# Blocked products over twelve chunks instead of eight, in a streaming attention step on one Trainium2 core

## What is computed

```python
z = einsum('bld,dc->blc', h, w_in)             # fq fk fv fg ff sq sk sv sg
fo = forgetting_attention(fq, fk, fv, lf) * silu(fg)       # 16 heads of 64
so = sliding_window_attention(sq, sk, sv, sinks, rel_bias) * silu(sg)   # 16 heads, 4 key/value heads
out = einsum('blc,cd->bld', concat([fo, so]), w_out)
y = layer_norm(ALPHA * h + out)
```

## Time and profile before

| | |
|---|---|
| median of 3 runs | 1018.74 us (1018.06 to 1019.41) |
| the profiled execution, its own time | 1019.1 us |
| its span in the trace | 1017.6 us, 1.5 us less than its time |
| TensorE busy | 998.6 us, 98% |
| VectorE busy | 715.2 us, 70% |
| ScalarE busy | 531.7 us, 52% |
| granted TensorE clock, mean | 0.996 of full speed |

### The profile page before, as it was taken

One profiled execution on the slowest core, in us unless ns is written; L12 is line 12 of the kernel. 1 busy time (PEld: TensorE's weight loads), 2 busy tenths in 40 slices (PEclk: granted clock), 3 DMA queues, 4 the chain that ended last, 5 costly groups with the idle time before them and its releaser, 6 DMA issues.

```text
span 1017.6 us, 20277 instructions
## 1 busy us (share of the span) xinstructions
PE 998.6 (98%) x7283; PEld 937.3 (92%) x7283; DVE 715.2 (70%) x1423; ACT 531.7 (52%) x1217; POOL 81.5 (8%) x156
## 2 busy tenths in 40 slices
PE   9999999999999999999999999999999999999995
PEld 6899999999999999999999999999999888888884
DVE  6988686776868677686767787668787655141685
ACT  5556465565645556464655676556677562111400
POOL 1620101001010100001010000000000000000000
PEclk9999999999999999999999999999999999999998
DMA  9142333223233323234321222231226443222423
GB/s 347 57 134 100 117 112 130 90 96 108 94 125 110 126 67 103 98 106 140 111 95 60 91 81 98 98 105 56 85 82 249 173 175 104 83 82 82 166 68 118
DMA packets 36258, 115.06 MB, mean 113 GB/s; under 512 B 9312, under 2 KB 9728, under 8 KB 33584
## 3 DMA queue, kind: packets, MB, share of 16 engines
q1 hardware_dynamic: 24208, 87.00, 24.8%
q0 software_dynamic: 11856, 27.14, 7.9%
q10 hardware_dynamic: 144, 0.26, 0.1%
HBM read 99.31 MB, written 18.29 MB: 116 GB/s over the span
## 4 chain that ended last, share of the span: by engine, by line
PE 86%; DVE 6%; DMA 4%; issue 2%; ACT 2%; SPq 1%; DVEq 0%; ACTq 0%
PE ps L1642 28%; PE ps L1652 25%; PE ps L1895 20%; PE ps L1860 5%; PE ps L1834 4%; DMA w_raw<-in_w_all 2%; PE ps L1818 2%; PE ps L1817 2%; DMA x_raw<-in_xT 2%; DVE wl L1118 1%; DVE tb L1295 1%; PE ps L1880 1%; SPq L582 0%; PE ps L1838 0%; ACT pt L961 0%
## 5 line engine op out<-in xcount | busy, mean ns | idle before, releaser
L1642 PE MATMUL ps<-xh,wh 128*128 128x296 f32 (+1 forms) x860 | 258.8, 301 | 0.2 <-DVE xl L1366 0.2
L1642 PE MATMUL ps<-xh,wl 128*128 128x296 f32 (+1 forms) x860 | 254.8, 296 | 0.0
L1642 PE MATMUL ps<-xl,wh 128*128 128x296 f32 (+1 forms) x860 | 254.6, 296 | 0.0
L1895 PE MATMUL ps<-wh,mix_parts 128*128 128x512 f32 x576 | 184.1, 390 | 0.0
L1642 PEld LDWEIGHTS ps<-xh,wh 128*128 128x128 f32 x860 | 161.8, 188 | 3.8 <-DVE xl L1366 1.8
L1642 PEld LDWEIGHTS ps<-xl,wh 128*128 128x128 f32 x860 | 161.9, 188 | 0.0
L1642 PEld LDWEIGHTS ps<-xh,wl 128*128 128x128 f32 x860 | 161.5, 188 | 0.0
L1118 DVE TENSOR_TENSOR wl<-w_raw,wh 128x1024 fp32r<-128x1024 f32 (+1 forms) x150 | 143.0, 953 | 19.8 <-ACT wh L853 8.5
L939 ACT ACTIVATE tb<-tb,small 128x256 f32<-128x256 f32 (+5 forms) x160 | 81.3, 508 | 92.2 <-DVE small L1314 64.2
L1895 PEld LDWEIGHTS ps<-wh,mix_parts 128*128 128x128 f32 x576 | 108.2, 188 | 22.3
L1895 PE MATMUL ps<-wl,mix_parts 128*128 128x512 f32 x320 | 124.5, 389 | 0.0
(11 more groups left out here) (198 smaller groups left out, 1737.3 us busy)
## 6 DMA issues: line engine op xcount, KB each, us to landing
w_raw<-in_w_all SPq DMA_DIRECT2D x106, 512.0 KB, 4.5
w_raw<-in_w_all SPq DMA_DIRECT2D x14, 1024.0 KB, 4.8
cbc<-c_rows POOLq DMA_DIRECT2D x16, 360.0 KB, 4.1
x_raw<-in_xT SPq DMA_DIRECT2D x7, 592.0 KB, 11.7
rows<-in_x_p POOLq DMA_DIRECT2D x4, 1024.0 KB, 5.2
out_y_p<-rows SPq DMA_DIRECT2D x16, 256.0 KB, 2.5
mix_rows<-mixT POOLq DMA_DIRECT2D x14, 288.0 KB, 2.4
rel_copies<-rel_rows POOLq DMA_DIRECT2D x8, 384.0 KB, 10.5
```

What stands on the lines that cost most here:

```text
L1642: ins = nc.tensor.matmul(ps[:, bank, result(tile, h)], a[f][:, w], b[:, ko, first:first + width], start=(ko == n_first and i == 0), stop=( ...
L1895: ins = nc.tensor.matmul(ps[:, bank, :], a, b[slot][:, w], start=(ko == 0 and i == 0), stop=(ko == KO - 1 and i == len(products) - 1))
```

## The change

The blocks now cover 12 chunks (CUT = 6) and 4 are plain. A block product has 18 matmuls and is issued as three pieces of 6; a plain unit has 6. A duo is still 15 units, in 29 pieces (UNIT_PIECES), and all steps are counted in pieces. The unit order after 7 changes: 8 is "four", 9 and 10 plain tile 0 late, 11 and 12 plain tile 1 early.

The x sums grow to 6 chunks each. Sum seven stays in SBUF; six and three share one buffer, `sum_both`: both are stored to DRAM in the opening and each is fetched again in every duo from 2 on, three after unit 1, six after unit 7. The first duo's loads of the next fronts come behind the landing of these two stores in SyncE's program.

Smaller edits: the forgetting attention's row terms (`cbc`) are loaded last among a stretch's loads; cached keys are cast at `steps - 14`; `make_seven` and `make_five` come before the low front; `back_parts(d, 0)` on VectorE moves into the next duo; one stretch in each sliding-window group is "late"; the relative bias is copied 32 times instead of 128 and loaded in four parts; the opening's gate steps are placed anew and `mid_part` and `last_part` take the gates' tanh.

```diff
+UNIT_PIECES = [3, 3, 3, 3, 1, 1, 3, 3, 3, 1, 1, 1, 1, 1, 1]
-CUT = KO // 4
+CUT = 3 * KO // 8
+REST = (KO - 2 * CUT) // 2
-GATES_TURNED_AT, V_FIRST_AT = 11, 14
+GATES_TURNED_AT, V_FIRST_AT = 24, 28
-BIAS_COPIES = FOX_PAIRS
+BIAS_COPIES, COPIES = FOX_PAIRS, CHUNK // 2
...
         elif len(duos) == 2:
-            score = [3 * i + 3 for i in range(5)]
+            score = [6 * i + 10 for i in range(5)]
         else:
-            score = [2 * i + 1 for i in range(5)]
-        turn = [x + 4 for x in score]
-        value = [turn[2], turn[2], turn[4], turn[4], score[4] + 5 if len(duos) < 2 else score[4] + 7]
+            score = [4, 7, 11, 14, 18] if late else [4 * i + 1 for i in range(5)]
+        self.lag = 1 if final else 2
+        turn = [x + (7 if late else 4 * self.lag) for x in score]
+        value = [turn[2], turn[2], turn[4], turn[4],
+                 score[4] + (5 if final else 10 if late else 11 if len(duos) < 2 else 14)]
...
+            sp.wait_ge(sum_low, 2)
+            sp.dma_start(sum_rows[0], sum_both[:].rearrange("p a b c -> p (a b c)")).then_inc(sums_stored, 16)
             sp.wait_ge(back_low[0], 1)
             load_part(2, 0, BACK, back_loaded)
+            sp.wait_ge(sum_low, 4)
+            sp.dma_start(sum_rows[1], sum_both[:].rearrange("p a b c -> p (a b c)")).then_inc(sums_stored, 16)
+            sp.wait_ge(sums_stored, 32)
...
-                sp.wait_ge(*((four_made, d) if f == 0 else (right_low, d)))
+                sp.wait_ge(*((four_made, d) if f == 0 else (five_low, d)))
...
+            def load_sums(i, used, loaded):
+                sp.wait_ge(unit_done, used)
+                sp.dma_start(sum_both[:].rearrange("p a b c -> p (a b c)"), sum_rows[i]).then_inc(loaded, 16)
+            def load_three(d):
+                load_sums(1, UNITS * (d - 1) + 2, three_loaded)
+            def load_duo(d):
+                load_next_front(d, 0)
                 load_next_front(d, 1)
-                load_next_front(d, 0)
                 load_next_back(d)
+                load_sums(0, UNITS * (d - 1) + 8, six_loaded)
                 sp.wait_ge(back_low[0], d + 1)
                 load_part(d + 2, 0, BACK, back_loaded)
...
# ScalarE
-                        if u == 7 and not last:
-                            front_parts(d + 1, (unit_done, st.after(k, 6)))
...
+                        if r == 24 and not last:
+                            seven_part(d + 1, (unit_done, st.after(k, 8)))
+                            six_part(d + 1, (unit_done, st.after(k, 7)))
...
+                    if inside and r == 18 and not last:
+                        front_parts(d + 1, (unit_done, st.after(k, 6)))
# VectorE
+            def last_sum():
+                dve.wait_ge(sum_high, 4)
+                low_of(both_low, x_raw[:, first_x, early], both_high, sum_low)
...
+                        if r == 2 and not st.first:
+                            back_parts(d, 0)
+                        if r == 6:
                             take_six(st, k)
+                            five_part(d)
+                        if r == 8:
+                            right_part(d)
+                        if r == 9:
                             take_seven(st, k)
+                            make_four(d, (unit_done, st.after(k, 2)))
...
-                            if u == 8:
-                                front_parts(d + 1)
-                            if u == 9:
+                            if r == 20:
                                 make_seven(d + 1, (unit_done, st.after(k, 7)))
                                 make_five(d + 1)
-                            if u == 10:
+                            if r == 21:
+                                front_parts(d + 1)
+                            if r == 22:
                                 make_six(d + 1)
-                            if u == 12:
+                            if r == 25:
                                 seven_part(d + 1)
                                 six_part(d + 1)
-                            if u == 14:
-                                back_parts(d + 1, 0)
...
-                    if st.first and s == GATES_TURNED_AT - 1:
+                    if st.first and s == GATES_TURNED_AT - 2:
                         keep_gates()
# TensorE
-                for j in range(CUT):
+                for j in range(2 * piece, 2 * piece + 2):
...
+                            pe.wait_ge(six_loaded, 16 * d - 16)
...
+                            pe.wait_ge(three_loaded, 16 * d - 16)
```

More of the change, by code:

```diff
@@ L153, in metas, with terms @@
     @staticmethod
+    def terms(g):
+        return 32 * g + 32
+    @staticmethod
     def metas(g, i):
@@ L191, in metas, with terms @@
     @staticmethod
+    def terms(g):
+        return 32 * FOX_PAIRS + 64 * (g - FOX_PAIRS) + 64
+    @staticmethod
     def metas(g):
@@ L216, in __init__ @@
         self.last, self.final = last, final
-        self.steps = OUT_STEPS if final else UNITS * len(duos)
+        self.steps = OUT_STEPS if final else PIECES * len(duos)
         if final:
@@ L485, in whole @@
                             g=first - 1, kvs=FOX_PAIRS + m, turn_before=first - 2 if m else None, keep=True))
-                with engine.Fori(first + 1, first + (4 if m == 0 else 3)) as g:
+                run(Stretch(["gq"], d0 + 2, own=Swa, pair=first + 1, kind=Swa, g=first,
+                            kvs=FOX_PAIRS + m + 1, turn_before=first - 1, keep=True, late=True))
+                with engine.Fori(first + 2, first + (4 if m == 0 else 3)) as g:
                     run(Stretch(["gq"], g + (d0 + 1 - first), own=Swa, pair=g, kind=Swa, g=g - 1,
@@ L804, in run @@
                                    ).then_inc(v_cached, 16)
+                    if st.own is Fox:
+                        pool.wait_ge(score_read, Fox.base(g))
+                        pool.sem_inc(pool_passed, 1)
+                        for head in range(2):
+                            pool.dma_start(cbc[:, head, :], c_rows[bass.ds(2 * g + head, 1), :]
+                                           .rearrange("a n -> (a n)").partition_broadcast(P)
+                                           ).then_inc(row_terms_loaded, 16)
                     if not st.keep:
@@ L1062, in run @@
-                        if last and u in (11, 12):
-                            act.wait_ge(unit_done, st.after(k, 10))
-                            mixed_high(u - 11)
-                    for i in st.at(st.score_at, s - 2):
+                        if r == 27 and last:
+                            weights_high(0, 0, 1, (unit_done, st.after(k, 10)), True)
+                        if last and r in (20, 23):
+                            act.wait_ge(unit_done, st.after(k, 6))
+                            mixed_high(r // 22)
@@ L1478, in run @@
                 for s in range(st.end + 1):
-                    k, u = divmod(s, UNITS)
+                    k, r = divmod(s, PIECES)
                     inside = k < len(st.duos)
                     ready = None
-                    for i in st.at(st.score_at, s - 2):
+                    if inside:
+                        d, last = st.duo(k), st.last and k == len(st.duos) - 1
+                    for i in st.at(st.score_at, s - 2 * st.lag):
                         reciprocals(st, i)
-                    if u == 0 and 1 <= k <= len(st.duos):
+                    if r == 0 and 1 <= k <= len(st.duos):
                         join(st, k - 1, 1, 1)
@@ L1715, in unit @@
                         pe.wait_ge(under_made, d)
-                    ins = plain(1, 1, duo[1], BOTTOM, range((u - 11) * CUT, (u - 10) * CUT), 2 * CUT)
-                ins.then_inc(unit_done, 1)
+                    ins = plain(1, 1, duo[1], BOTTOM, rest(u - 13), 2 * CUT)
+                if piece == UNIT_PIECES[u] - 1:
+                    ins.then_inc(unit_done, 1)
             def opening_products():
```

301 lines of the change are left out of this document (156 added, 145 removed).

## The result

The changed kernel takes 1040.14 us (median of 4 runs, 1038.82 to 1040.43), the kernel before 1018.59 in the same session. The ratio is 1.0208, 95% interval 1.0194 to 1.0222: slower by 2.1%, where 1013.0 was forecast. The spans of the profiled executions are 1038.9 and 1017.6 us.

A forecast was written before the change was run, and what follows sets the result against it. TensorE's instruction stream was taken to bound most stages, VectorE being full in duo 1. 1019.1 - 20.4 + 9 + 3.2 + 1.6 + 0.8 = 1013.3 profiled, so 1013.0 us median; range 1001 to 1024.

The forecast's parts named there:

- the upper bounds of the parts: Largest losses allowed: opening 11, two-duo stretches 1.1 in each of eight, late 2.4 each, four one-duo 0.6 each, sliding-window 0.6.
- What is removed: Six fewer matmuls in each of 25 duos, 150 at 0.136 us: 20.4 us saved, the whole gain.
- The opening: Through duo 2: larger sums, a late store and fronts queued behind it delay TensorE; loss 9 us, bounds 2 and 11.
- The two-duo stretches: Eight forgetting-attention stretches: second turn worked out as 1.1 us late, bounds zero and 1.1; 0.4 taken each, 3.2 in all.
- The chain: VectorE's work from second duo's sum seven to next stretch's first scores: 18.0 us, so scores are taken up at 10.2.
- VectorE's chain decides: Rival: late take-up costs 1.1 in eight stretches, 2.4 in two, 0.6 in four, opening 9; 1023.3 us, chance 0.19.
- The late stretches: Two late one-duo stretches: first scaled rows up to 2.4 us late for TensorE; 0.8 taken each, 1.6 for both.
- The other one-duo stretches: Four stretches: second kept turn at most 0.6 us late for the values; 0.2 taken each, 0.8 together.
- Sums fetched in turn: Fetches of three and six hidden, three having 10.7 us for 7.2; uncovered, each us late costs 1 in 24 duos.
- The rest: Row terms last, cached keys, bias copies and loads, and mixed rows for the end: taken to cost nothing.
- The output projection: The last 223 us of the kernel, taken as not touched by the change.
- The clock rival: Waiting in the opening brings 1.2 GHz, costing 3 us more: 1016 to 1019; chance 0.11 together with other small losses.

The follow-up runs named there:

- more_before: Changed kernel plus one unused VectorE reduction in each of nine two-duo stretches, in the first duo just ahead of the first scores; 1047.4 us.
- more_after: Changed kernel plus the same unused VectorE reduction, as often, but in the second duo, behind the scores and ahead of sum seven; 1038.9 us.
- three_first: Changed kernel with SyncE asking for sum three before it waits for VectorE's low back; 1038.4 us.
- scores_12: Changed kernel with score, turn and first value steps two steps later in two-duo stretches (scores at 12, 18, 24, 30, 36); 1034.5 us.
- scores_three: Changed kernel with the edits of both scores_12 and three_first; 1018.2 us.
- less_vector: Changed kernel with VectorE's weight sums and low parts and the casts of seven and four covering 512 of 768 columns from duo 2 on; 1018.4 us.
- best_even: later_steps, but with the late stretches' scores at 3, 7, 11, 15, 18; 1009.9 us.
- later_steps: scores_three plus fronts_first, late stretches' scores at 6, 9, 13, 16, 19, and the second half of the first output weights one step sooner; 1026.0 us.
- later_values: later_steps with the values of the first two tiles one step later in the one-duo stretches; 1026.5 us.
- small_fetch: Changed kernel with each fetch of a sum cut to 296 of 3552 columns, 148 KB in place of 1776 KB; 1039.0 us.
- best: later_steps with the late stretches back at scores 4, 7, 11, 14, 18; 1013.7 us.
- filled: Changed kernel plus unused matmuls in the opening, 18 before the wait for the gates' sums and 38 before the first turned values; 1041.3 us.
- fronts_first: Changed kernel with duo 2's two fronts asked for before the second store, and the wait for the stores just before the first fetch of six; 1036.2 us.

## Why the prediction was wrong, point by point

The forecast was 27.1 us too low, and the measured time lies 16 above the upper end of the range, 1024. No choice within its bounds would have reached it: the upper bounds of the parts (11, 8.8, 4.8, 2.4 and 0.6) add up to 27.6 us, and 41.7 were lost. One of them doesn't follow from its own row: 360 KB in 4.1 us makes 20.2 us of 1776 KB, and the opening's bound 22, not 11.

**What is removed** was right: 150 matmuls fewer at an unchanged 0.136 us; a stretch without waits is 58.17 us against 58.05.

**The opening** was right in mechanism and near in size, 6.9 against 9. The chain went as forecast: last sum stored at 56.2 (57.0 was worked out), the fronts asked for behind it at 62.16 (64.2), VectorE's sum seven waiting for them. VectorE's timeline in after:

```profile
54.20 2.00 DVE L1169 TENSOR_TENSOR sum_both<-x_raw,sum_both 128x1776 fp32r<-128x1776 f32 x1
...
69.02 0.96 DVE L1185 TENSOR_TENSOR w_sum<-w_raw 128x768 f32<-128x768 f32 x1 [3.37 <-DMA w_raw<-in_w_all]
...
73.82 0.16 DVE L1520 COPY cq<-ps 64x16 f32<-64x16 f32 x1
```

The gates came at 73.9 (75.0), and TensorE's first turned values at 74.13. Its wait there was 3.0 and not 5.9, as TensorE, at 1.2 GHz from 66 on, came to it at 71.1 and not 69.1; so the low clock was paid inside a wait that would have been there anyway. The store took 5.9 us (56.23 to 62.16), shorter than the 7.2 taken from the rows.

**The two-duo stretches are the step that failed.** The prediction worked out that the scores would be taken up at 10.2 and the second turn be 1.1 late, and then chose 0.4 us a stretch, "nearer to what before shows". 0.4 became 2.3. Four things were wrong in it.

The choice: it rests on "the turn of before would just miss too, and it didn't". It did. Only the stretch at 249.35 had been read; in three of the eight stretches of before TensorE waited at the second turn:

```profile
389.28 1.05 PE L1834 MATMUL ps<-ident,tb 128*128 128x128 f32 x6 [1.13 <-ACT tb L951]
...
449.55 1.05 PE L1834 MATMUL ps<-ident,tb 128*128 128x128 f32 x6 [0.20 <-ACT tb L951]
...
510.00 0.96 PE L1834 MATMUL ps<-ident,tb 128*128 128x128 f32 x6 [0.38 <-ACT tb L951]
```

Those stretches took 61.2, 60.3 and 60.4 us. A turn with nothing to spare was no reason to discount the sum; it meant that a further microsecond would show, as more_before and more_after demonstrate.

The turn: the wait that costs most in after is the first turn's, not the second's (1.17 and 0.24 us behind the pace in three_first, where the fetch doesn't cover them). ScalarE's timeline in after, up to the first turn, whose transposes start at 276.58:

```profile
274.50 0.19 ACT L977 ACTIVATION_READ_ACCUMULATOR tb<-tb,small 128x1 f32 x1
274.59 0.83 ACT L922 ACTIVATE wh<-w_sum 128x768 fp32r<-128x768 f32 x1
275.68 0.23 ACT L960 ACTIVATE v_twice<-vT 128x32 f32<-128x32 f32 x1 [0.26 <-DVE vT L1277]
275.82 1.32 ACT L989 ACTIVATE tb<-tb,small 128x512 f32<-128x512 f32 x2
```

The exp of the first scores ends at 274.7; the cast of sum four and a copy that waits for VectorE's join stand before the scaling, 1.1 us that the prediction, with its eye on the second turn, didn't weigh. In before that copy came behind the scaling (261.94 against 260.40).

The chain: 18.0 was 18.8, so take-up was at 11.0.

And the fetch: three was taken to be issued at 4.9 us and came at 8.5, because the step queued ahead of it on SyncE, the wait for VectorE's low back, was itself among the steps that had moved later (`back_parts(d, 0)` into the next duo). In after this adds nothing, since the chain alone costs the 2.3; it is why repairing the chain alone (scores_12) gave 5.7 us and not 17.

The rival "VectorE's chain decides" had the mechanism with a chance of 0.19 and the price 1.1: too small by half, for the 0.8 of chain and for what stands before the first turn.

**The late stretches** (1.6 taken, bound 4.8, measured 10.2) were outside their bounds. The bound looked at the first scaled rows alone; the spacing of the turns was left out. Shown is that the repairs of the other stretches give back 1.0 and 0.7 us (34.5 and 35.2 in scores_three), wider steps 1.9 and 2.0 more, and a lighter VectorE 1.9 (33.57 in less_vector against 35.5); what holds best_even's 32.6 and 32.9 against 30.6 is open, and so is which part of later_steps cost its 6 to 7 us.

**The other one-duo stretches** lost 0.7 to 1.1 each and not 0.2. Of that some 0.5 is a shown wait for the turned sample rows (`pt_meta`); later_values took it from the values and put one of up to 1.3 us before the next turn, so what these stretches would need stays open.

**Sums fetched in turn**: hidden, said the text, and "if that cover goes, each us late costs 1 us". Neither held: in after the cover was gone, and taking the fetch's wait away alone (small_fetch, three_first) gave 1.1 and 1.8 us in all, because another wait ended at the same place. The rest, row terms, cached keys, bias, shows in no wait of TensorE.

**The output projection**, taken as untouched, lost 2.6. VectorE's last join begins 1.63 us after its start (815.88 against 814.25) where before it was 0.20 (795.78 against 795.58):

```profile
814.74 1.23 DVE L1165 TENSOR_TENSOR wl<-w_raw,wh 128x1024 fp32r<-128x1024 f32 x1 [0.64 <-ACT wh L881]
815.88 0.46 DVE L1277 TENSOR_TENSOR last_part<-ps,last_part 128x296 f32<-128x296 f32 x1
```

A low part of the first output weights, whose cast on ScalarE went from 4.1 us before that border to 0.6 before it, stands ahead of the join. One step sooner for both, in best, took the gap at the first scores from 2.1 to 1.0 and the stage to 222.0. The other 1.5 or so is the clock (last section).

**The clock rival** happened in the opening and cost under 1 us there by filled; the 1.5 us of the output projection it didn't foresee.

## What to carry to other kernels

When a chain by your own sum just misses, take the miss at its full size: an engine with 20% idle time can still be full on the one stretch between its last release and the deadline, and there nearly all of an added microsecond is paid. Read every repeat of a stage before you say that it has no wait: here five of eight had none. Work out a DMA's issue time through every wait queued ahead of it, the moved ones above all. And never subtract a wait from the profile as a gain: take away two that lie side by side, each alone and both, before you say what either costs.

## What the runs showed of the hardware

The idle time shown before a matmul understates the loss, by 0.16 us per interruption here (0.47 shown, 0.63 lost), so stages have to be compared by starts. DMA durations depend on company: with the sums' fetches cut to 148 KB, `cbc` took 4.3 us in place of 8.8 and a front of 768 KB 5.8 in place of 7.5, and in that kernel no stage but the opening became shorter for it. And the granted clock after a gap is not set by the length of that gap alone: behind the same shown 2.1 us at the start of the output stage, the mean clock in after was 0.68 of full speed in 818:822 and 0.89 in 822:826, so part of them ran at 1.2 GHz (its output stage 224.65 us), while fronts_first stayed at 1.00 through the same stretch (223.09).
